# One kernel of a two-layer trunk: the first MLP gets the structure of the second, and the modulation vectors are summed elsewhere

## What is computed

```
cs = silu(c)                                        # 1024 values
mod = cs @ ada_w[layer] + ada_b[layer]              # 6 vectors of 1024 a layer
kv_mod = cs @ kv_ada_w + kv_ada_b                   # 2 more: SH_KV, SC_KV
u = h * (1 + scale) + shift
y = mlstm_mixer(u, ...)  or  attention(...)
h = layer_norm(ALPHA * h + (1 + g_m) * y, ln_g, ln_b)
u = h * (1 + sc_f) + sh_f
y = square(relu(u @ mlp_w_up)) @ mlp_w_down         # 1024 -> 4096 -> 1024
h = layer_norm(ALPHA * h + (1 + g_f) * y, ln_g, ln_b)
```

## Time and profile before

| | |
|---|---|
| runs | 2146.18, 2149.24, 2151.24 us; median 2149.24 |
| profiled execution | 2148.5 us, its span 2146.8 us |
| TensorE | 98% of the span busy, 9816 matmul records |
| DVE, ACT, POOL | 70%, 41%, 13% |
| loads through stage | 248 of 512 KB, 3.6 us from issue to landing |
| granted clock of TensorE | 0.997 in the mean |

### The profile page before, as it was taken

The page is one execution under the profiler, slowest core; times in us unless marked ns, Lnnn a source line. Parts: engine busy times, 40 slices in busy tenths (PEclk is TensorE's granted clock), DMA queues, the critical chain, the costliest instruction groups (busy, mean ns, idle before and its releaser), DMA issues.

```text
span 2146.8 us, 28666 instructions
## 1 busy us (share of the span) xinstructions
PE 2100.7 (98%) x9816; PEld 1702.2 (79%) x9816; DVE 1502.8 (70%) x2343; ACT 882.8 (41%) x1529; POOL 270.6 (13%) x248
## 2 busy tenths in 40 slices
PE   6999999999999999999999999999999999999998
PEld 5888888878888888888888777678787888888886
DVE  7423666678676676776768665767788788778878
ACT  4201454162234233342337455655434434534552
POOL 0000220010010110110100023232000011011034
PEclk9999999999999999999999999999999999999999
DMA  7434643303424224224121210211345433533531
GB/s 298 137 102 126 124 94 139 126 20 120 126 69 137 97 79 137 78 83 147 34 98 72 79 30 11 79 58 42 124 182 185 162 131 137 205 114 121 195 137 79
DMA packets 77315, 242.16 MB, mean 113 GB/s; under 512 B 8417, under 2 KB 8593, under 8 KB 73649
## 3 DMA queue, kind: packets, MB, share of 16 engines
q1 hardware_dynamic: 69376, 219.18, 30.1%
q0 software_dynamic: 5088, 17.48, 3.7%
q10 hardware_dynamic: 2768, 4.41, 0.5%
HBM read 225.29 MB, written 15.76 MB: 112 GB/s over the span
## 4 chain that ended last, share of the span: by engine, by line
PE 84%; DVE 7%; DMA 4%; ACT 3%; issue 2%; POOL 1%; SPq 0%; DVEq 0%; ACTq 0%; POOLq 0%
PE ps L2670 25%; PE ps L2672 25%; PE ps L2671 25%; DMA stage<-in_stream 3%; PE ps L3135 1%; PE ps L3165 1%; PE ps L3149 1%; DVE wlo L1609 1%; ACT whi L964 1%; PE ps L2914 1%; PE ps L2773 1%; PE ps L2899 1%; DMA early_place<-in_early 1%; PE ps L2903 1%; DVE stats L1918 1%
## 5 line engine op out<-in xcount | busy, mean ns | idle before, releaser
L2672 PE MATMUL ps<-uhi,wlo 128*128 128x512 f32 x760 | 296.4, 390 | 0.0
L2670 PE MATMUL ps<-whi,uhi 128*128 128x512 f32 x704 | 287.6, 408 | 0.2 <-ACT resid L1309 0.2
L2670 PE MATMUL ps<-uhi,whi 128*128 128x512 f32 x704 | 276.3, 392 | 5.9 <-DVE wlo L1609 3.2
L2672 PE MATMUL ps<-whi,ulo 128*128 128x512 f32 x704 | 275.4, 391 | 0.0
L2671 PE MATMUL ps<-wlo,uhi 128*128 128x512 f32 x704 | 274.8, 390 | 0.0
L2671 PE MATMUL ps<-ulo,whi 128*128 128x512 f32 x704 | 274.8, 390 | 0.0
L2672 PEld LDWEIGHTS ps<-uhi,wlo 128*128 128x128 f32 x760 | 143.1, 188 | 29.8
L2670 PEld LDWEIGHTS ps<-uhi,whi 128*128 128x128 f32 x704 | 132.6, 188 | 37.0 <-DVE wlo L1609 4.6
L2670 PEld LDWEIGHTS ps<-whi,uhi 128*128 128x128 f32 x704 | 132.5, 188 | 36.6 <-issue 10.0
L2672 PEld LDWEIGHTS ps<-whi,ulo 128*128 128x128 f32 x704 | 132.2, 188 | 28.9
L2671 PEld LDWEIGHTS ps<-ulo,whi 128*128 128x128 f32 x704 | 132.5, 188 | 27.2
(11 more groups left out here) (437 smaller groups left out, 4614.6 us busy)
## 6 DMA issues: line engine op xcount, KB each, us to landing
stage<-in_stream SPq DMA_DIRECT2D x248, 512.0 KB, 3.6
hlo<-ulo_dram SPq DMA_DIRECT2D x28, 1024.0 KB, 4.8
ulo<-ulo_dram SPq DMA_DIRECT2D x20, 1024.0 KB, 5.3
w_whole<-in_stream SPq DMA_DIRECT2D x14, 512.0 KB, 5.2
aux<-in_early SPq DMA_DIRECT2D x8, 512.0 KB, 7.5
early_place<-in_early SPq DMA_DIRECT2D x8, 512.0 KB, 14.2
resid<-in_xt SPq DMA_DIRECT2D x8, 512.0 KB, 15.7
resid<-in_x POOLq DMA_DIRECT2D x8, 512.0 KB, 9.7
```

Source lines behind the costliest of these rows:

```text
L2670: pe.matmul(dst, left_hi, right_hi, start=start, stop=False, skip_group_check=more)
L2672: return pe.matmul(dst, left_lo, right_hi, start=False, stop=stop, skip_group_check=more)
```

## The change

The first MLP runs the code of the second. `mlp_chunk`, `mlp_loads`, `both_chunk`, `mlp_sums` and `mlp_through` take the number m of the MLP, and `seven_chunk` and the quarter sums are gone. In chunk 0 of both, the up weights w2 and w3 are loaded and split first (`CHUNK_LOADS`, `LOADS_AT`). POOL adds the bias row to all eight residual tiles of the last chunk, of which DVE had four. w96 and w97 are loaded after the first MLP; DVE's part of them, and three modulations, stand between the last up half and the last downs (`before_tail`); `angles` moves into the last chunk.

The products of the seven vectors and of SH_F0, SC_F0, SH_KV move to the stages QK, V, O1 and OUT0. For 62 of them the block is loaded into a side place: four in the part of qk that is written late, in pieces of 1 KB, later scratch and two rows of lnrows. Each vector has a total of its own (acc or gate_row) and is summed by `sum_vector` in bank 6 or 7. SP's list up to the end of V is written by `issue_order`.

At the first chunk of seven products, SP issues the down rows b12 and b22 ahead of the ring loads P4 and P2.

```diff
+BESIDE_QK = {6: [(SH_F0, 0, 4)], 7: [(SH_F0, 4, 8)], 8: [(SC_F0, 0, 4)], 9: [(SC_F0, 4, 8)], 10: [(SH_KV, 0, 4)],
+             11: [(SH_KV, 4, 8)], 12: [(SC_KV, 0, 4)], 13: [(SC_KV, 4, 8)]}
+BESIDE_V = [[(SH_M1, 0, 3)], [(SH_M1, 3, 6)], [(SH_M1, 6, 8), (SC_M1, 0, 1)], [(SC_M1, 1, 4)], [(SC_M1, 4, 7)],
+            [(SC_M1, 7, 8), (G_M1, 0, 2)], [(G_M1, 2, 5)], [(G_M1, 5, 6)], [(G_M1, 6, 8)], [(SH_F1, 0, 1)],
+            [(SH_F1, 1, 2), (SC_F1, 0, 1)], [(SH_F1, 2, 3), (SC_F1, 1, 3)], [(SH_F1, 3, 4), (SC_F1, 3, 4)],
+            [(SH_F1, 4, 5), (SC_F1, 4, 6)], [(SH_F1, 5, 6), (SC_F1, 6, 8)], [(SH_F1, 6, 8)]]
+BESIDE_O1 = {t: (G_F1, t - 4, t - 3) for t in range(4, 8)}
+BESIDE_OUT0 = {0: (G_F1, 4, 5), 1: (G_F1, 5, 6), 2: (G_F1, 6, 7), 3: (G_F1, 7, 8), 4: (G_F0, 0, 2), 5: (G_F0, 2, 4),
+               6: (G_F0, 4, 6), 7: (G_F0, 6, 8)}
...
-CHUNK_LOADS = [4, 5, 2, 3, 6, 7, 8, 9]
+CHUNK_LOADS = [2, 3, 4, 5, 6, 7]
+LOADS_AT = {2: (2,), 3: (3, 4), 4: (5,), 5: (6,), 6: (7,)}
...
+        if t == T - 1:
+            w(30, 31)
+        ada(*BESIDE_OUT0[t])
...
+def issue_order():
+
+
+    taken = [("w", w) for w in range(6)]
+    for w in range(6, 14):
+        taken += [("w", w)] + [("ada", vec, k) for vec, first, end in BESIDE_QK[w] for k in range(first, end)]
+    for tile in range(2 * T):
+        taken += [("w", w) for w in ((14, 15) if tile == T - 1 else ())]
+        taken += [("ada", vec, k) for vec, first, end in BESIDE_V[tile] for k in range(first, end)]
+        taken += [("w", w) for w in ((7 + tile,) if tile in (T + 1, T + 2) else ())]
+    out = []
+    for x in taken:
+        if x[0] == "ada" and in_side(*x[1:]):
+            n = SIDE.index(x[1:])
+            later = [m for m in range(n + 1, len(SIDE)) if SIDE_SLOT[m] == SIDE_SLOT[n]]
+            if later:
+                out.append(("side", later[0]))
+        elif NUMBER[x] + 2 < AFTER_V:
+            out.append(("turn", NUMBER[x] + 2))
+        if x == ("w", 2):
+            out += [("side", n) for n in range(4)]
+        if x == ("w", 11):
+            out += [("side", 24), ("side", 25)]
+        if x == ("ada", SH_KV, 6):
+            out.append(("side", 26))
     return out
...
+        def side_place(slot):
+
+            if slot < 4:
+                half, col = slot % 2, 2 * HALF - 4 * P + slot // 2 * 2 * P
+                return qk[:, 4 * half:4 * half + 4, col:col + 2 * P]
+            part = scratch[:].rearrange("p a n -> p (a n)") if slot == 4 else lnrows[:, slot - 5, :]
+            return part.rearrange("p (a n) -> p a n", a=4)
...
+            def load_side(n):
+
+                former = [x for x in range(n) if SIDE_SLOT[x] == SIDE_SLOT[n]]
+                if former:
+                    sp.wait_ge(side_used, former[-1] + 1)
+                elif SIDE_SLOT[n] < 4:
+                    sp.wait_ge(early_sum, K)
+                else:
+                    sp.wait_ge(gate_m, 6)
+                    sp.wait_ge(gate_v, 11)
+                    sp.wait_ge(side_used, max(x for x in range(n) if SIDE_SEM[x] == SIDE_SEM[n]) + 1)
+                dst = side_place(SIDE_SLOT[n])
+                src = stream[SIDE_BASE + n]
+                sp.dma_start(dst, src.rearrange("p (a n) -> p a n", a=4)).then_inc(side_in[SIDE_SEM[n]], 16)
...
-            for n in range(4):
-                store_sum(n)
-            after(first, 0, 0)
-            sp.wait_ge(sum_lo_stored[0], 32)
-            ring_load("P4")
-            sp.wait_ge(sum_lo_stored[2], 32)
-            down_row("b12", 0, 0)
-            down_row("b22", 0, 0)
-            ring_load("P2")
...
+                    store_sum(m, n)
+                sp.wait_ge(sum_lo_stored[2], 32 * (m + 1))
+                down_row(m, "b12", 0, 0)
+                down_row(m, "b22", 0, 0)
+                after(first, 0, 0)
+                sp.wait_ge(sum_lo_stored[0], 32 * (m + 1))
+                ring_load("P4")
+                ring_load("P2")
...
+                pool.dma_start(lnrows[:, 1, :], consts["ln_b"][2 * m].partition_broadcast(P)).then_inc(rows_in, 16)
+                pool.wait_ge(rows_ready, (2, 5)[m])
+                pool.wait_ge(dve_evac, DVE_BEFORE[first])
+                for t in range(T):
+                    if t == T // 2:
+                        pool.wait_ge(group_done, first + 14)
+                    pool.tensor_tensor(resid[:, t, 0:D], resid[:, t, 0:D], lnrows[:, 1, :],
+                                       ALU.add).then_inc(h_by_pool, 1)
+
...
+            def preps_and_parts(w):
+                preps(w)
+                for part in BESIDE_QK[w]:
+                    adas(*part)
...
+            for tile in range(2 * T):
+                nh, t = divmod(tile, T)
+                if tile == T - 1:
                     preps(14, 15)
-                evac_v(0, t)
-            for t in range(T):
-                evac_v(1, t)
-                adas(SH_KV, range(t, t + 1))
-                if t == 0:
-                    take_mod(SC_F0)
-                if t in (1, 2):
-                    preps(15 + t)
-                if t == 4:
+                evac_v(nh, t)
+                for vec in {0: (SH_KV,), 2: (SC_KV,), 4: (SH_M1,), 8: (SC_M1,), 10: (G_M1,)}.get(tile, ()):
+                    take_mod(vec)
+                for part in BESIDE_V[tile]:
+                    adas(*part)
+                if tile in (T + 1, T + 2):
+                    preps(7 + tile)
...
-            v.wait_ge(x_in, 16 * T)
+            v.wait_ge(resid_in, 16 * T)
             for t in range(T):
                 if t == T - 1:
                     preps(30, 31)
                 add_out(FIRST["out0"] + t, t, 0, ALPHA)
-                if 1 <= t < T - 1:
-                    adas(G_F0, ((0,), (1,), (2, 3), (4,), (5, 6), (7,))[t - 1])
+                adas(*BESIDE_OUT0[t])
+                if t == 6:
+                    take_mod(G_F1)
             modulation(1, SC_F0, SH_F0, ln=0)
...
+            def before_tail():
+
+                preps(96, 97)
+                modulation(2, SC_KV, SH_KV, ln=1)
+                modulation(3, SC_M1, SH_M1, ln=1)
+                modulation(4, SC_F1, SH_F1, ln=2)
+
+            mlp_through(0, tail_kv, between=before_tail)
...
             def sum_vector(vec):
 
+                total, bank = total_of(vec), SUM_BANK.get(vec, M)
                 if vec == SC_M0:
                     pe.wait_ge(early_sum, K)
+                elif in_side(vec, K - 1):
+                    pe.wait_ge(side_used, SIDE.index((vec, K - 1)) + 1)
                 else:
                     pe.wait_ge(loads_used, NUMBER["ada", vec, K - 1] + 1)
-
-                    pe.wait_ge(sum_read, SUM_NUMBER[vec])
+                if vec != SC_M0:
+                    pe.wait_ge(sum_read, SUM_NUMBER[vec] - (1 if vec in SUM_BANK else 0))
                 for k in range(K):
-                    last = pe.matmul(ps[:, M, k:k + 1], acc[:, k * P:(k + 1) * P], ones[:, 0:1], start=True, stop=True)
-                last.then_inc(sum_done, 1)
-
...
-            def sum_quarters(i, used):
-
-                pe.wait_ge(loads_used, used)
-                pe.wait_ge(sum_read, SUM_NUMBER[SC_KV] + i)
```

1634 lines of the change are left out of this document (702 added, 932 removed).

## The result

The changed kernel takes 2171.34 us in the median of four runs (2169.49 to 2173.89), the kernel before 2147.99 of four (2146.18 to 2151.24). The ratio is 1.0108 with a 95% interval of 1.0090 to 1.0125: slower, on the other side of the forecast 2139.5 and 18 us above its range. The profiled execution has a span of 2170.1 us, 23.3 more than before.

The account below looks back on a forecast made before the run. TensorE, busy 98% of the span, was taken to bound the kernel through its matmul count and its idle time. 2148.5 less gains of 54.2 plus costs of 45.4 gave 2139.7, forecast 2139.5 us, range 2106 to 2153.

Parts of the forecast that it names:

- What the change gives: Gains (a) to (e), mainly first-MLP chunks running like the second's and fewer matmuls: 54.2 us in sum.
- (d): Chunk 0's up weights split one step earlier, over both MLPs: TensorE's wait and half clock go, gain 5.0 us.
- (f): Seven vectors summed by 8 one-column matmuls each on TensorE instead of in quarters: cost 11.9 us, not hidden.
- the slack terms: Costs (g) to (l), where moved work uses up little slack at the seams: 33.5 us in all.
- (h): V to O0: w18 issued behind SH_F1's last product, and two sums stand there: cost 1.3 us, between 0 and 3.
- (l): First MLP's last chunk and tail: angles, w96/w97 halves and modulations on DVE delay evacuations: cost 7.3 us, bounds 0 and 10.
- (g): Start of QK: four side loads ahead of w5 and w6 make w6 late: cost 2.8 us, bounds 0 and 5.
- (k): First chunk of seven products, both MLPs: TensorE waits for ring P4 behind down rows: cost 14.0 us, bounds 5 and 17.
- the queue rule named there: In (k): DMA engines take one queue's descriptors in ring order, so P4 comes wholly behind the down rows, 4.7 us wait.
- (j): OUT0 to OUT1: w30 and w31 loads stand behind later G_F0 products, norms queued behind: cost 5.0 us, bounds 0 and 7.
- (i): Entry of the output gate and OUT0: a sum and a product now stand ahead: cost 3.1 us, bounds 0 and 5.
- The rival on the slower side: Moved products in V wait for their loads, over 0.3 us on average in tiles of three: 2174 us, chance 0.12.

Follow-up runs that it names:

- the two runs that tried: G_F1's products beside O1, against the changed kernel: 2184.44 us; one G_F0 product less ahead of w30 and w31, against the kernel with six edits: 2139.92 us.
- four details undone here: Changed kernel with ring P4 first, angles before P2, DVE adding half the bias rows, and side loads behind w6: 2137.80 us, ratio 0.9958 to the kernel before.

## Why the prediction was wrong, by its own steps

What the change gives came in: 76.25 us a period, seven times 24 matmuls, and 5.9 us at the two up stages (1.2 and 4.7) where (d) had 5.0. So did (f), 1.84 us a sum at the full clock, seven more of them. The error is in the slack terms: worked out at 33.5 us, they were 65.6, which is 77.5 less the 11.9 of (f).

- **(h), V to O0: 1.3 forecast, 14.2 measured** (21.0 less four sums). This is the largest failure, and it failed as a step: it asked what stands ahead of w18 on SP's queue and not what else uses the DMA engines in that window. Behind two POOL issues there SP's loads take 9 to 11 us. In the kernel before only one load was issued soon behind the same broadcasts, 4.1 us after the first; it took 6.9, and nothing stood for it. Of the 14.2, TensorE's idle time is 6.3 (8.1 against 1.8) and the half clock behind it 3.3 (the sum 1.7, eight matmuls 1.6); the rest is not split up, and with the loads partly out of the way 9.4 are left.
- **(l), last chunk and tail: 7.3 forecast, 17.3 measured.** The collision with POOL was in the sum for the two low halves (2.8 each; they took 2.95). For the small operations I took 0.2 from a row where POOL stood still. The working also puts the evacuation at 2106, where 8.0 behind 2096.82 is 2104.8; the rest has no row. The angles took 9.2 us, not 2.5, and the first modulation 2.30, not 0.2. Not foreseen at all was that the same edit costs the second MLP 3.0 us at its end, where DVE had added half of the rows.
- **(g), QK: 2.8 forecast, 8.6 measured** (12.0 less two sums), of which the run that moves the side loads takes back 5.5 to 5.9. w6 was split at 60.20, where the forecast had 60.2, and TensorE waited 2.24. The rest is the clock: the 16 small matmuls took 2.91 us instead of 1.85, and 10 more ran at half pace. The forecast gave this 1.6 us to long waits only. There is one more such stretch at 117 us, seven matmuls, with no wait before it; neither it nor the rest of the 8.6 is explained.
- **(k), first chunk of seven: 14.0 forecast, about 16 measured** (2.1 and 0.7 us for P7, 4.3 and 3.9 for P4, 2.2 us of half clock each). The mechanism and the wait of 4.7 were right; by the queue rule named there P4 came wholly behind the down rows, and the trace agrees: they land at 609.10 and 610.33, P4 at 613.48. In the first MLP P7's low half was 2.1 us late, not the 0.65 of the forecast.
- **(j), OUT1: 5.0 forecast, 6.5 measured; (i): 3.1 and 3.9.** Right in place and near in size; OUT1 is 3.7 to 6.1 over the kernel before in traces of the same code. What sets it is not settled by the two runs that tried.

These losses and the 3.0 at the end of the second MLP make some 69; gains that the forecast did not have (1.7 us between the MLPs, 0.9 more at the up stages, 0.9 at the start, 0.7 in the first MLP's chunk 0) bring them to within 1 us of the 65.6. Put into the forecast's sum for its 33.5, they give 2148.5 - 54.2 + 11.9 + 65.6 = 2171.8. The bounds given for (g), 0 to 5, (h), 0 to 3, and (l), 0 to 10, did not hold either, which is why the range failed. They came from the duration of one load and of single operations, not from rows where two engines or two queues meet. One number of the working is wrong without any effect on the sum: the products that leave the MLP are 56 (seven vectors of eight), not 62, which is the number of loads into side places.

The rival on the slower side gave 2174 for products that wait for their loads in V. The time is near, but the mechanism was only half right: its condition (over 0.3 us a product in tiles of three) was met in many tiles without harm, and one tile held the loss, by a cause that the rival did not name.

## What to carry to other kernels

Work moved off a full engine goes into windows that others use: for each move list every transfer and every operation of the other engines in that window, and price it from a row where both run together. A small operation is not cheap beside a busy POOL, and a load is not 3.6 us just behind a broadcast. When a change is slower, try its parts one at a time before giving it up: four details undone here turned 1.1% slower into 0.4% faster, and another placing of the work at the end of V into 0.8%.
